# Two sorted expert layers: the two experts that run alone move from rounds two and three to rounds four and five of nine

## The reference

```python
    aff = jax.nn.sigmoid((xf @ router_w).astype(jnp.float32))
    ...
    local = lax.top_k(biased[tok, g_sel], TOP_K)[1]
    expert = g_sel[:, None] * EXPERTS_PER_GROUP_2 + local
    ...
    def expert_block(args):
        xb, e = args
        hid = jax.nn.silu(xb @ w_gate[e]) * (xb @ w_up[e])
        return hid @ w_down[e]
```

## Time and profile before

| what | us |
|---|---|
| median of 3 runs (1864.61 to 1866.58) | 1864.75 |
| the profiled execution's own time | 1866.2 |
| its span, first to last instruction | 1864.4 |
| PE busy | 1694.4 (91%) |
| expert stretch of `e`: first transfer after the order, to PE's last scatter | 1213.3 to 1453.2 |
| expert stretch of `o`: the same | 1612.1 to 1850.7 |

### The profile page before, as it was taken

One profiled execution on the slowest core, in us unless ns is written; L12 is line 12 of the kernel. 1 busy time (PEld: TensorE's weight loads), 2 busy tenths in 40 slices (PEclk: granted clock), 3 DMA queues, 4 the chain that ended last, 5 costly groups with the idle time before them and its releaser, 6 DMA issues.

```text
span 1864.4 us, 20556 instructions
## 1 busy us (share of the span) xinstructions
PE 1694.4 (91%) x8053; PEld 982.3 (53%) x8053; DVE 761.8 (41%) x1621; ACT 398.7 (21%) x761; POOL 92.8 (5%) x144
## 2 busy tenths in 40 slices
PE   8999989999799998899886999799998788799995
PEld 5587754343456776444335876444443564454342
DVE  1678742221356766222116356532221644512223
ACT  1232321111022232111103355011110341111111
POOL 1111100000110110000001000000000100000000
PEclk9999979999899999899997999799999899799998
DMA  9868599999974875799996521497999741679995
GB/s 380 343 236 323 226 330 410 421 421 421 420 295 149 321 272 215 316 422 421 421 423 255 194 78 67 182 360 284 423 421 423 277 181 67 263 291 383 421 422 240
DMA packets 83739, 578.84 MB, mean 310 GB/s; under 512 B 8896, under 2 KB 13232, under 8 KB 28336
## 3 DMA queue, kind: packets, MB, share of 16 engines
q1 hardware_dynamic: 60624, 500.20, 66.2%
q0 software_dynamic: 16416, 63.97, 9.1%
q10 hardware_dynamic: 6592, 13.20, 2.1%
HBM read 574.13 MB, written 3.20 MB: 310 GB/s over the span
## 4 chain that ended last, share of the span: by engine, by line
PE 73%; DMA 15%; DVE 7%; ACT 2%; issue 2%; SPq 0%; POOL 0%; POOLq 0%; DVEq 0%; ACTq 0%
PE bank L767 70%; DMA ring<-in_weights 12%; DMA hi_ring<-in_weights 2%; PE bank L799 2%; DVE mix L1943 1%; DVE work L1801 1%; ACT work L1388 1%; DMA consts<-in_cst 1%; ACT mix L1388 1%; DVE mix L1801 1%; DVE small L1801 1%; PE bank L895 0%; DVE oT L1979 0%; DVE x L1801 0%; DVE small L1952 0%
## 5 line engine op out<-in xcount | busy, mean ns | idle before, releaser
L767 PE MATMUL bank<-ring,work 128*64 128x512 f32 (+2 forms) x1516 | 390.5, 584 | 23.7 <-DMA ring<-in_weights 22.3
L1388 ACT ACTIVATE work<-bank 128x512 f32<-128x512 f32 (+6 forms) x234 | 123.4, 531 | 831.6 <-PE bank L767 427.1
L767 PEld LDWEIGHTS bank<-ring,work 128*64 128x64 f32 (+2 forms) x1516 | 141.4, 144 | 252.7 <-issue 243.4
L767 PE MATMUL bank<-ring,oT 128*64 128x512 f32 (+1 forms) x864 | 221.2, 596 | 11.0 <-DMA ring<-in_weights 9.0
L1801 DVE TENSOR_TENSOR work_parts<-bank,work_parts 128x512 fp32r<-128x512 f32 x68 | 47.0, 692 | 370.6 <-ACT work_parts L1388 370.6
L767 PE MATMUL bank<-work_parts 128*128 128x256 f32 (+2 forms) x612 | 151.5, 357 | 21.6 <-DVE work_parts L2029 18.9
L767 PE MATMUL bank<-hi_ring,work 128*64 128x512 f32 (+1 forms) x608 | 154.3, 596 | 7.5 <-DMA hi_ring<-in_weights 6.0
L767 PEld LDWEIGHTS bank<-ring,oT 128*64 128x64 f32 (+1 forms) x864 | 76.1, 144 | 137.4 <-issue 136.8
L767 PEld LDWEIGHTS bank<-work_parts 128*128 128x128 f32 x612 | 108.2, 205 | 70.5 <-issue 37.8
L2118 DVE SCALAR_TENSOR_TENSOR work<-bank,small,work 128x512 f32<-128x512 f32 x34 | 25.5, 751 | 282.7 <-PE bank L767 213.6
L767 PE MATMUL bank<-ring,xT 128*128 128x512 f32 (+2 forms) x352 | 139.0, 554 | 1.7 <-DVE xT L2261 1.7
(11 more groups left out here) (236 smaller groups left out, 2052.2 us busy)
## 6 DMA issues: line engine op xcount, KB each, us to landing
ring<-in_weights SPq DMA_DIRECT2D x244, 1024.0 KB, 15.2
hi_ring<-in_weights SPq DMA_DIRECT2D x118, 1024.0 KB, 16.0
ring<-in_weights SPq DMA_DIRECT2D x52, 2048.0 KB, 10.5
hi_ring<-in_ada POOLq DMA_DIRECT2D x38, 512.0 KB, 11.8
mod_rows<-in_ada POOLq DMA_DIRECT2D x25, 512.0 KB, 6.1
work<-in_ada POOLq DMA_DIRECT2D x22, 512.0 KB, 6.1
hi_ring<-in_weights SPq DMA_DIRECT2D x5, 2048.0 KB, 10.6
work<-in_vecs POOLq DMA_DIRECT2D x8, 1024.0 KB, 7.5
```

What stands on the lines that cost most here:

```text
L767: ins = nc.tensor.matmul(o, lhsT, rhs, start=start, stop=stop)
L1388: return nc.scalar.activation(o, i, f, **kw)
```

## The change

One line: in `rounds_of` the rounds of `e` and `o` come in another order.

```diff
--- before
+++ after
 def rounds_of(tag):
     pair = [(p, p + 1) for p in range(0, NEXP, 2)]
-    return [pair[0], (2,), (3,), *pair[2:]] if tag in SORTED else pair
+    return [pair[0], *pair[2:4], (2,), (3,), *pair[4:]] if tag in SORTED else pair
```

## The result

| kernel | median us (runs) | ratio to before, 95% interval |
|---|---|---|
| before, beside the first measurement | 1864.68 (1861.08 to 1866.58) | 1 |
| changed, first measurement | 1848.12 (1845.73 to 1851.1) | 0.9911 [0.9898, 0.9923] |
| changed, second | 1849.48 (1847.58 to 1852.89) | 0.9925 [0.9912, 0.9939] |
| changed, third | 1850.37 (1847.82 to 1852.98) | 0.9930 [0.9917, 0.9944] |

The account below looks back on a forecast made before the run. PE was taken as the bound, waiting 15.4 us for weights in the two expert stretches; gains of 7.1 us in e and 6.4 in o gave 1864.75 - 13.5 = 1851.3 us, range 1849 to 1857.5.

Parts of the forecast that it names:

- a shallower hole: Layer e's weight transfers: a dip in rate near 1310 to 1345, shallower than the old one of 276 GB/s.
- one wait per layer, at d8.0: First down piece of round 8, layer e: the only weight wait left, 1.3 us; for o 0.6 us left.
- The least early lead: Second down piece of round 1, layer e: weights land 5.2 us before PE wants them, least of the early rounds.
- the term for the turns: PE's turns straight behind a scatter: cost 0, at most 2.8 us if VectorE came late.
- The interval of the shallow queue: Queue with little ahead, as at the restart: one piece lands every 5.3 us, taken between 4.98 and 5.5.
- The rule weighed in the prediction: Skill's advice for large transfers: 1 MB takes 6.15 us; as restart interval, 2.3 us left per layer, gain 10.8.
- That is 15.4 us in all: PE's listed waits for weights in both expert stretches, 8.4 us in e plus 7.0 in o; the most to gain.
- Half of the stall staying: Ring fills again behind the moved singles, about half the waits remain: 7.7 us gained, 1857 us; chance 0.10.
- the stall only moving: Singles block the ring as much wherever they stand, the end starves as before: 1864.75 us, no change; chance 0.05.
- The starved restart: Queue starts empty on heavy rounds, PE waits early; 1873.8 us if 18 us later than taken; chance 0.03.
- Its turning point: L is how many us later the queue restarts than taken; from L = 14 the change loses against the old order.
- The slow clock that would add to it: An idle PE granted 1.2 GHz, so a piece of a pair would take twice as long; not seen at 1.3 us waits.

Follow-up runs that it names:

- the old order with the quarter transfers: Kernel before, but layer o's transfers from round 1 on bring only a quarter of each matrix's columns, so PE need not wait: 1856.55 us, 0.9959.
- late restart: SP's first transfer of round 1 held back until PE releases three pieces more, in the kernel before: 1863.44 us, 0.9994; in the changed kernel: 1857.0 us, 0.9961.
- o alone: Kernel before with the new order given to layer o only, e keeping the old one: 1856.44 us, 0.9955.
- e alone: Kernel before with the new order given to layer e only, o keeping the old one: 1856.79 us, 0.9959.
- rounds six and seven: Changed kernel with the singles two rounds later still, in both layers: 1849.91 us, 0.9925 against the kernel before.
- three and four pieces held back: Changed kernel with SP's first transfer of round 1 held until PE releases three or four pieces more: 1857.0 us (0.9961) and 1875.66 us (1.0059).
- new order with quarter transfers: Changed kernel, but layer o's transfers from round 1 on bring only a quarter of each matrix's columns: 1849.07 us, 0.9920 against the kernel before.

## Why the forecast came out low

**What held.** PE bounds the stretches, and its waits for weights were what could be won: with the waits gone in one layer, that layer's stretch fell to the floor and the other's stayed. The queue at full rate to about 1300, then a shallower hole (338 GB/s, where 1310 to 1345 was named), one wait per layer, at d8.0, and all the hand-overs behind a scatter free. The least early lead was worked out as 5.2 us at d1.1. In the changed kernel its second transfer goes out at 1242.91 and lands 11.9 us later, at 1254.8; PE's row at 1254.37 holds three pieces without a wait, g2.1, d1.0 and d1.1:

```profile
1254.37 10.52 PE L767 MATMUL bank<-ring,work 128*64 128x512 f32 x48
...
1300.04 2.42 PE L767 MATMUL bank<-work_parts 128*128 128x512 f32 x8
1302.29 0.60 PE L799 MATMUL bank<-consts,work 128*128 128x128 f32 x4
```

```profile
1210.85 0.36 SPq L2683 DMA_DIRECT2D ring<-in_weights  x1
1211.41 0.34 SPq L2683 DMA_DIRECT2D ring<-in_weights  x1
...
1214.43 0.33 SPq L2683 DMA_DIRECT2D ring<-in_weights  x1
...
1242.91 0.33 SPq L2683 DMA_DIRECT2D ring<-in_weights  x1
```

```profile
ring<-in_weights SPq DMA_DIRECT2D x1, 1024.0 KB, 7.3
...
ring<-in_weights SPq DMA_DIRECT2D x1, 1024.0 KB, 9.2
...
ring<-in_weights SPq DMA_DIRECT2D x1, 1024.0 KB, 11.9
```

PE wants d1.1 two pieces on, at 1254.37 + 2 x 3.51 = 1261.4, a lead of 6.6 us for the 5.2 forecast. The scatter at 1300.04 is followed by the turn at 1302.29 with no wait for VectorE, so the term for the turns was rightly 0.

**The interval of the shallow queue** was a little too long. I took 5.3 us for a piece at the restart, from three pieces that landed 5.5 us apart. In the changed kernel the second transfer of g1.0 landed at 1211.41 + 7.26 = 1218.67, that of g1.1 at 1214.43 + 9.21 = 1223.64 (the view rounds to 7.3 and 9.2): 4.97 us for 2 MiB, although the queue had been empty. Up to d1.1 the mean is (1254.78 - 1218.67) / 7 = 5.16 us. Left over were 0.60 and 0.69 us, not 1.3 and 0.6, together 0.6 us more gain. By the prediction's own bounds, 0 left with 4.98 and 1.3 with 5.3, the shorter interval would do this; no run varies it alone. The rule weighed in the prediction, 6.15 us for 1 MB by the Trainium skill (DMA: Bandwidth & Descriptors, section Bandwidth, measured there on transfers issued from GpSimd), asked for 2.3 us of waits per layer; the trace does not agree, for transfers that follow each other in SP's queue land closer than that even in the first pieces after a pause.

**The step that failed** is the size of the term "That is 15.4 us in all", which was also the ceiling, "so 15.4 us at most", and with it the low end of the range. I read the time lost to a wait as its listed idle time. It is more. Pieces of layer o in the kernel before, then the same pieces in the old order with the quarter transfers:

```profile
1799.31 3.60 PE L767 MATMUL bank<-hi_ring,oT 128*64 128x512 f32 x16
1803.99 3.65 PE L767 MATMUL bank<-ring,oT 128*64 128x512 f32 x16 [1.08 <-DMA ring<-in_weights]
...
1823.86 3.65 PE L767 MATMUL bank<-hi_ring,oT 128*64 128x512 f32 x16 [1.30 <-DMA hi_ring<-in_weights]
1828.83 3.65 PE L767 MATMUL bank<-hi_ring,work 128*64 128x512 f32 x16 [1.32 <-DMA hi_ring<-in_weights]
```

```profile
1798.94 3.60 PE L767 MATMUL bank<-hi_ring,oT 128*64 128x512 f32 x16
1802.38 3.60 PE L767 MATMUL bank<-ring,oT 128*64 128x512 f32 x16
...
1819.04 3.60 PE L767 MATMUL bank<-hi_ring,oT 128*64 128x512 f32 x16
1822.47 3.60 PE L767 MATMUL bank<-hi_ring,work 128*64 128x512 f32 x16
```

With a wait of 1.32 us listed, 1828.83 - 1823.86 = 4.97 us pass from start to start; without one 1822.47 - 1819.04 = 3.43. The wait costs 1.54, which is 0.22 more than listed: the row ahead of it is listed with 3.65 us, though without a wait the next row starts 3.43 behind it. I had used that overlap for the length of a round and not for the waits. (The 3.51 of the prediction is the mean of a piece followed by a piece and one followed by a scatter; within a run of pieces it is 3.43 to 3.49.)

The two kernels keep the same distances up to the first wait, 1799.31 - 1607.42 = 191.89 us and 1798.94 - 1607.07 = 191.87. From there to the last scatter it is 1849.47 - 1799.31 = 50.16 against 1840.73 - 1798.94 = 41.79. So all of the 8.4 us arise where the six waits stand; 7.05 were listed, which is 0.22 too little for each. The floor says what there was in all: (244.6 - 234.9) + (243.25 - 234.9) = 9.7 + 8.4 = 18.1 us, not 15.4. Counted by steps, the 16.9 us of the stretches are 13.5 forecast and 0.7 for the smaller rest (15.47 listed before, 1.29 now, 14.2); the 2.7 that remain are 0.22 for each of the twelve waits that are gone, as in the run without waits. With 18.1 as the ceiling the low end would have been 1864.75 - 18.1 = 1846.65, and 1848.12 inside.

That the first measurement fell below the range is in part its scatter: the median of all 15 executions of the changed kernel is 1849.43, 0.4 us above the range's low end. That the ceiling was set too low is not.

**What stays open.** The stretches give 16.9 us in the first two traces and 16.2 by the means over all traces of a layer in the old or the new order (without the late restart of the new order and without layer o of the quarter transfers); the three measurements gave 16.6, 14.0 and 13.0, and their intervals overlap only from 14.4 to 15.5. Part of the difference lies between e and o, in code that the change doesn't touch. Its length in the twelve traces, with the granted clock of that stretch (old order in e: before, late restart, o alone, old order with quarter transfers; singles later in e: the changed kernel three times, e alone, rounds six and seven, three and four pieces held back, new order with quarter transfers):

| order in e | us between e and o | granted clock |
|---|---|---|
| old | 154.3, 155.6, 155.3, 153.0; mean 154.5 | 0.87, 0.86, 0.86, 0.88 |
| singles later | 153.1, 156.4, 156.2, 155.6, 155.7, 156.2, 156.5, 156.1; mean 155.7 | 0.88, 0.85, 0.85, 0.86, 0.85, 0.85, 0.85, 0.85 |

Windows of the changed kernel's first trace and then of its third:

```profile
1442.00:1595.00 153.00, 116.87 (x575) 86.03 (x577) 81.28 (x238) 46.84 (x108) 9.77 (x12) 0.88 0.44 170
```

```profile
1440.00:1596.00 156.00, 119.34 (x573) 87.17 (x573) 81.69 (x238) 46.80 (x108) 9.75 (x12) 0.85 0.43 168
```

The longer time goes with the lower granted clock, and 0.85 appears in six of the eight traces with the singles later in e and in none of the four others. So the new order seems to give back about 1 us there; 16.2 - 1.2 = 15.0 lies within the 14.4 to 15.5 of the measurements. Twelve traces are few, and no run shows why the clock would be lower there.

**The rivals.** Half of the stall staying and the stall only moving are out: 0.6 and 0.7 us of waits. The starved restart doesn't occur in the change, but it is real. Its turning point was put at L = 14: with L = 10.6 the new order still gains 0.39%, with L = 21.2 it loses 0.59%. Its size per microsecond was set too high: for L = 10.6 it gives some 5.4 us of waits per layer, and 3.6 and 4.6 were listed; it rests on the interval of 5.3, which was too long. The old order takes the same late restart for nothing (0.9994), for it wasted that time anyway: that is the price of the change, a start with less to spare. The slow clock that would add to it came with four pieces held back, and not at waits of 1.3 us. The Trainium skill (TensorE: Matmul & The Clock Gate, Part 1) has an idle PE at half clock; the run with the 5.64 us wait agrees, with 9.94 us for two pieces.

## What to carry to other kernels

Where rounds that ask little of the transfer queue stand among rounds that ask much, put them where the buffer has been partly drained: at the start they only fill a ring that is full already, and the queue's lost time returns at the end as waits. The exact place matters little (rounds four and five or six and seven gave the same time), but work out first how late the queue may restart before the heavy rounds starve. Price a wait by the distance from start to start against pieces that don't wait, and take the ceiling of a gain from a run with the wait's cause removed, not from the listed idle time.

## What was not expected of the hardware

Listed idle time of PE ahead of a row of matmuls was 0.22 us short of what the wait cost (1.32 listed, 1.54 lost). On a queue that had been empty, 1 MiB transfers issued in pairs landed the second piece of 2 MiB 4.97 us behind the first, and the first eight 5.16 us apart on average. After 5.64 us without work PE's next two pieces took 9.94 us for 7.0, while waits of 1.3 us left the granted clock at 1.00.
